# Head norm of the prompt moved from the last stage into the sample mLSTM; decode with two score banks and one pair of key banks

## The chip, the core and the metric

The kernel runs on one core of one Trainium2 chip. The metric is the device time of one execution in microseconds; the median of three runs stands for the kernel. A profile of one execution goes with it: every instruction with its engine, its start and its duration. PE is TensorE, DVE VectorE, ACT ScalarE, POOL GpSimd, SP SyncE, whose queue starts the DMAs.

## What is computed

One step of a hybrid decoder layer. A prompt of 512 tokens (16 learned meta tokens before it) and 8 decode sequences of 4 tokens pass one input projection. Half of the width goes to 8 heads of differential attention (the decode sequences read 32 pages of 128 old keys and values each), half to 4 heads of an mLSTM with a matrix memory. Each head's output is normed, the mLSTM heads are gated, then come the output projection with a residual and an MLP:

```python
def mlstm_output(h, og, g):
    B, T = h.shape[:2]
    hn = rms_norm(h, g)
    o = jax.nn.sigmoid(og.astype(jnp.float32)).reshape(B, T, N_HEADS_M, HEAD_DIM_M)
    return (hn * o).reshape(B, T, MLSTM_WIDTH).astype(og.dtype)

def finish_layer(x, a_heads, m_out, lam_init, attn_out_norm, w_out, norm_ffn, w_up, w_down):
    B, T, _ = x.shape
    a = (rms_norm(a_heads, attn_out_norm) * (1.0 - lam_init)).reshape(B, T, ATT_WIDTH)
    x = x + jnp.concatenate([a.astype(x.dtype), m_out.astype(x.dtype)], axis=-1) @ w_out
    hf = rms_norm(x, norm_ffn) @ w_up
    return x + jnp.square(jax.nn.relu(hf)) @ w_down
```

Here `m_out` is the normed head times the sigmoid of its gate `og`, and `rms_norm` divides by the root of the mean square over a head's 128 (attention) or 256 (mLSTM) values and multiplies by a gain.

## The kernel before

The kernel is a row of stages with a barrier between them: setup, input projection, prompt attention, mLSTM features, prompt mLSTM, `sample_mlstm`, `decode_attention`, `finish_and_project`, `mlp`, `emit`. Each engine has its own list of instructions in a fixed order; semaphores (`wait_ge`, `then_inc`) tie them together. All activations lie transposed, features on partitions and tokens in columns; `mix` holds the 16 chunks of 128 features of all heads (8 attention chunks, then two for each mLSTM head). A matmul with full precision is three passes, low part times high, high times low, high times high (`exact_passes`), so every operand is split into a leading and a trailing part, by ScalarE and VectorE.

`sample_mlstm` runs over the four mLSTM heads for the decode sequences. SP loads four heads' inputs and states (lines 1293 to 1297), then writes the new states as they come (line 1301). For each head TensorE makes the numerators with 16 matmuls of two passes each (`sums`, L1426), then updates the states with 16 more (L1458), which VectorE adds (L1379). ScalarE takes the absolute value of the denominator (L1402), VectorE divides (`divide`, L1348 to L1354), TensorE turns the result back.

`decode_attention` goes through 128 slots of two pages (the loop variable `s`) and some more to drain. In a slot TensorE transposes the keys of page 2s in two halves of four heads each (`turn(s, 0, 0)`, `turn(s, 0, 1)`, L1627), multiplies values of nine slots before (`values`, L1677 to L1688), sometimes transposes probabilities (L1703) and makes the factors (L1713, L1720), transposes page 2s+1 (`turn(s, 1, ...)`) and makes the scores of slot s-1 (`scores`, L1645 to L1650). ScalarE copies the transposed keys out as leading part (`k_high`, L1928), VectorE subtracts for the trailing part (`k_low`, L1770). VectorE also reads the upper half of the scores with their bias (`take`, L1780), ScalarE the lower half (`slower`), GpSimd adds both (`take_slow`, L1608) and makes the trailing part of the values (`v_low`, L1599). The keys' transposes go to four PSUM banks, a pair for each page of a slot; the scores have one. The order on VectorE in a slot:

```python
                if s < PAIRS:
                    k_low(s, 0, 0)
                if 2 <= s < PAIRS + 2:
                    take(s - 2)
                if s < PAIRS:
                    k_low(s, 0, 1)
                ...
                if s < PAIRS:
                    k_low(s, 1, 0)
                    k_low(s, 1, 1)
                if done:
                    cut(v // PPU)
```

Between the second and the third come the trailing part of the probabilities (L1805) and, once a sample, the mixers (L1859); behind the last, in one slot of four, `cut` and `keep` (L1818, L1825), and at times a copy of the queries (L1759, L1764).

`finish_and_project` squares all 16 chunks on VectorE (L2167), sums them over partitions on TensorE (L2231), takes the root on ScalarE and the reciprocal on VectorE (L2183), spreads the inverse over the partitions on TensorE (L2241), multiplies (L2194) and splits (L2127, L2187) chunk by chunk; the gates are loaded and their sigmoid taken meanwhile (L2119, L2173). Only then does the output projection begin (L69 to L71, from `pe_tile`), tile by tile of 128 output features. After the split SP loads the residual over `mix` (L2067); the first tile's sum is added to it.

## Time and profile before

| | us |
|---|---|
| median of 3 runs | 3865.28 |
| lowest and highest | 3864.36, 3869.47 |
| the profiled execution | 3864.66 |
| its span in the trace | 3862.6 |
| mean granted clock of TensorE | 0.959 |

Busy over the span: PE 3595.9 us (93%), DVE 1808.7 (47%), ACT 1280.9 (33%), POOL 713.8 (18%). Times in the rows below are counted from the span's start. A busy PE is not a PE at its peak, as matmuls overlap; a granted clock of 1.00 is 2.4 GHz, 0.50 is 1.2 GHz.

### The profile page before, as it was taken

To read this page: it belongs to the slowest core of one execution; us is meant where nothing else is said; L and a number is where in the kernel's file an instruction comes from. 1 tells how busy PE (TensorE), PEld (TensorE's weight loads), DVE (VectorE), ACT (ScalarE), POOL (GpSimd) and SP (SyncE) were. 2 spreads that over 40 slices of the span, in tenths; PEclk is the share of its full clock that TensorE was granted. 3 is DMA by queue.
4 is the path that set the end of the run, shared out by engine and by line. 5 is a ranking of instruction groups with operands and counts; after the bars stand their busy time and mean duration, and the time that the engine had idled before them with its cause. 6 is when DMAs were issued, how large, how long until landed. Compare 5 with 4: busy or idle time off the path is not lost. (4 is left out here: it accounts for less than half of the span.)

```text
span 3862.6 us, 65521 instructions
## 1 busy us (share of the span) xinstructions
PE 3595.9 (93%) x26234; PEld 3328.7 (86%) x26234; DVE 1808.7 (47%) x2749; ACT 1280.9 (33%) x1879; POOL 713.8 (18%) x436
## 2 busy tenths in 40 slices
PE   7999998866789999999977999999999999999998
PEld 7999996545658888888846999999999999999998
DVE  4222223764447777777765343333333333333333
ACT  3111111432107777777752232222222222222221
POOL 0000000000005888888870000000000000000000
PEclk9999999768869999999988999999999999999999
DMA  7443332115548899999964322222222222222221
GB/s 206 111 111 106 105 107 87 51 53 170 115 152 315 319 327 328 331 326 329 327 210 124 87 75 88 88 88 88 88 88 88 88 88 88 88 88 88 88 88 58
DMA packets 454169, 564.77 MB, mean 146 GB/s; under 512 B 39462, under 2 KB 330196, under 8 KB 453388
## 3 DMA queue, kind: packets, MB, share of 16 engines
q1 hardware_dynamic: 453932, 561.47, 45.3%
q8 instruction: 166, 2.72, 0.3%
q14 instruction: 71, 0.58, 0.0%
HBM read 514.93 MB, written 46.47 MB: 145 GB/s over the span
## 5 line engine op out<-in xcount | busy, mean ns | idle before, releaser
L1599 POOL TENSOR_TENSOR dc_vl<-dc_vpages,dc_vh 128x1024 fp32r<-128x1024 f32 x256 | 609.0, 2395 | 19.0 <-ACT dc_vh L1928 18.6
L69 PE MATMUL f_acc<-hidden_hi,ffn_lo 128*128 128x272 f32 x2048 | 591.7, 289 | 2.8 <-DVE mix_t L2353 2.8
L71 PE MATMUL f_acc<-xf_hi,ffn_hi 128*128 128x272 f32 x2048 | 594.1, 290 | 0.0
L71 PE MATMUL f_acc<-hidden_hi,ffn_hi 128*128 128x272 f32 x2048 | 592.9, 290 | 0.0
L69 PE MATMUL f_acc<-xf_hi,ffn_lo 128*128 128x272 f32 x2048 | 591.0, 289 | 1.0 <-DVE xf_lo L2375 0.4
L70 PE MATMUL f_acc<-hidden_lo,ffn_hi 128*128 128x272 f32 x2048 | 590.7, 288 | 0.0
L70 PE MATMUL f_acc<-xf_lo,ffn_hi 128*128 128x272 f32 x2048 | 588.5, 287 | 0.0
L69 PE MATMUL z_acc<-xn_hi,win_lo 128*128 128x280 f32 x1536 | 447.6, 291 | 1.1 <-DVE win_lo L302 1.1
L71 PE MATMUL z_acc<-xn_hi,win_hi 128*128 128x280 f32 x1536 | 448.5, 292 | 0.0
L2304 ACT ACTIVATE ffn_hi<-ffn_raw 128x2048 fp32r<-128x2048 f32 x127 | 242.3, 1908 | 619.4 <-PE f_acc L71 619.4
L70 PE MATMUL z_acc<-xn_lo,win_hi 128*128 128x280 f32 x1536 | 447.3, 291 | 0.0
L1770 DVE TENSOR_TENSOR dc_kl<-dc_pk,dc_kh 128x512 fp32r<-128x512 f32 x512 | 337.7, 681 | 151.9 <-ACT dc_kh L1928 151.4
L69 PEld LDWEIGHTS f_acc<-hidden_hi,ffn_lo 128*128 128x128 f32 x2048 | 384.5, 188 | 6.4 <-DVE mix_t L2353 6.4
L69 PEld LDWEIGHTS f_acc<-xf_hi,ffn_lo 128*128 128x128 f32 x2048 | 385.7, 188 | 4.3 <-DVE xf_lo L2375 3.6
L70 PEld LDWEIGHTS f_acc<-xf_lo,ffn_hi 128*128 128x128 f32 x2048 | 386.6, 189 | 0.0
L70 PEld LDWEIGHTS f_acc<-hidden_lo,ffn_hi 128*128 128x128 f32 x2048 | 386.0, 188 | 0.0
L71 PEld LDWEIGHTS f_acc<-xf_hi,ffn_hi 128*128 128x128 f32 x2048 | 385.4, 188 | 0.0
L71 PEld LDWEIGHTS f_acc<-hidden_hi,ffn_hi 128*128 128x128 f32 x2048 | 384.9, 188 | 0.0
L2358 DVE TENSOR_TENSOR ffn_lo<-ffn_raw,ffn_hi 128x2048 fp32r<-128x2048 f32 x127 | 291.2, 2293 | 150.8 <-ACT ffn_hi L2304 150.8
L2353 DVE TENSOR_TENSOR mix_t<-mix_t,f_acc 128x544 f32<-128x544 f32 x256 | 182.9, 720 | 362.1 <-PE f_acc L71 362.1
L1928 ACT ACTIVATE dc_kh<-dc_pk 128x512 fp32r<-128x512 f32 x512 | 278.4, 596 | 127.3 <-PE dc_pk L1627 126.3
L69 PEld LDWEIGHTS z_acc<-xn_hi,win_lo 128*128 128x128 f32 x1536 | 289.4, 188 | 1.3 <-DVE win_lo L302 1.3
(359 smaller groups left out, 6248.8 us busy)
## 6 DMA issues: line engine op xcount, KB each, us to landing
dc_kpages<-in_cache_k SPq DMA_DIRECT2D x256, 512.0 KB, 5.4
dc_vpages<-in_cache_v SPq DMA_DIRECT2D x256, 512.0 KB, 5.2
ffn_raw<-in_w_up SPq DMA_DIRECT2D x64, 1024.0 KB, 6.4
ffn_raw<-in_w_down SPq DMA_DIRECT2D x64, 1024.0 KB, 5.0
win_raw<-in_w_in SPq DMA_DIRECT2D x48, 1024.0 KB, 6.1
ffn_raw<-in_w_out SPq DMA_DIRECT2D x16, 1024.0 KB, 6.3
z_scratch<-z_out SPq DMA_DIRECT2D x48, 280.0 KB, 2.4
sm_c<-in_state_C SPq DMA_DIRECT2D x32, 256.0 KB, 4.5
```

The lines of the kernel that those rows point to most:

```text
L69: nc.tensor.matmul(out, wlo, xhi, start=first, stop=False)
L70: nc.tensor.matmul(out, whi, xlo, start=False, stop=False)
L71: return nc.tensor.matmul(out, whi, xhi, start=False, stop=last)
L1599: G.tensor_tensor(vl[:, m % VBUF, :], vring[:, m % RING, :], vh[:, m % VBUF, :].bitcast(F32), ALU.subtract).then_inc(vlo, 1)
L1770: V.tensor_tensor(kl[:, k, hs, i * P:(i + 1) * P], pk[i][half][:, :].rearrange("p (h t) -> p h t", h=HH), kh[:, k, hs, i * P:(i + 1) * P]. ...
L1928: A = lambda out, x, **more: nc.scalar.activation(out, x, ACT.Copy, **more)
L2304: nc.scalar.activation(flow.hi[:, i % 2, :], flow.raw[:, i % G, :], ACT.Copy).then_inc(flow.hi_made, 1)
L2353: nc.vector.tensor_tensor(halves(xt[:, oc, :]), halves(xt[:, oc, :]), acc[2 + i % 2][:, :, 0:d.ohalf], ALU.add).then_inc(added, 1)
L2358: nc.vector.tensor_tensor(flow.lo[:, i % 2, :], flow.raw[:, i % G, :], flow.hi[:, i % 2, :].bitcast(F32), ALU.subtract).then_inc(flow.lo_m ...
```

## The change

In the sample stage the squares, the sums over partitions, the inverse root, the gates and the multiplication by gain and inverse are now done for the 512 columns of the prompt. The inverse goes to DRAM and comes back spread over the partitions by 12 broadcast DMAs. `num` has one bank instead of two, to make room for the sums. In the last stage only the 32 columns of the decode sequences are normed; the split goes over the first half of the columns and then the second; the first weight tile is loaded first; the residual comes in four pieces. In the decode the scores go to two banks in turn, and a slot's two pages share one pair of key banks.

```diff
@@ sample_mlstm
+                if h == 1:
+                    for i in range(d.hm):
+                        sp.dma_start(og[i][:, :, :], ogv[cog // E + i][:, :, N_META:TP]).then_inc(og_in[i], 16)
...
             for h in range(d.hm):
+                if h == d.hm - 1:
+                    sp.wait_ge(inv_made, 1)
+                    sp.dma_start(inv_dram, inv[:, :]).then_inc(inv_out, 16)
+                    sp.wait_ge(inv_out, 16)
+                    for i in range(NH):
+                        sp.dma_start(spread[:, i, :], inv_dram[i:i + 1, :].to_broadcast([P, S])).then_inc(spread_in, 16)
...
+            def gate(h):
+                dve.wait_ge(sigmoid_made, h + 1)
+                dve.wait_ge(squared, d.ha + (h + 1) * E)
+                x = prompt[:, d.ha + h * E:d.ha + (h + 1) * E, :]
+                V.tensor_tensor(x, x, og[h][:, :, :], ALU.mult).then_inc(gated, 1)
+
+            def invert():
+                dve.wait_ge(gathered, d.kc)
+                V.tensor_scalar(root[:, :], mean[0:NH, 0:S], EPS, None, ALU.add).then_inc(rooting, 1)
+                dve.wait_ge(rooted, 1)
+                V.reciprocal(inv[:, :], root[:, :]).then_inc(inv_made, 1)
...
+                V.scalar_tensor_tensor(prompt[:, n, :], prompt[:, n, :], gain, spread[:, head(n), :],
+                                       ALU.mult, ALU.mult).then_inc(normed, 1)
...
+                if h == d.hm - 2:
+                    invert()
+                    for i in range(d.hm):
+                        gate(i)
                 dve.wait_ge(state_new, E * NB * (h + 1))
                 V.tensor_copy(nbh(ncols[:, :, :])[:, :, :, h], c0[h][:, :, :, MD]).then_inc(new_put, 1)
+            for n in range(d.kc):
+                norm(n)
...
+                for n in part(h):
+                    if n >= 6:
+                        act.wait_ge(gathered, n - 5)
+                    nc.scalar.activation(sq[n % 6][:, :], prompt[:, n, :], ACT.Square).then_inc(squared, 1)
...
-                if h >= 2:
-                    pe.wait_ge(divided, h - 1)
+                if h:
+                    pe.wait_ge(divided, h)
...
+                for n in part(h):
+                    pe.wait_ge(squared, n + 1)
+                    pe.wait_ge(gather_made, 3)
+                    x = head(n)
+                    nc.tensor.matmul(mean[0:NH, 0:S], gather[:, int(n >= d.ha), NH - 1 - x:2 * NH - 1 - x], sq[n % 6][:, :],
+                                     start=(n == 0), stop=(n == d.kc - 1)).then_inc(gathered, 1)
@@ decode_attention
-        pk = [[ps(f"dc_pk{i}{half}", [P, 512]) for half in range(2)] for i in range(2)]
+        pk = [ps(f"dc_pk{half}", [P, 512]) for half in range(2)]
-        pscore = ps("dc_pscore", [P, 512])
+        pscores = [ps(f"dc_pscore{i}", [P, 512]) for i in range(2)]
...
-                if n >= 2:
-                    pe.wait_ge(klo, 2 * n - 3 + half)
+                if n >= 1:
+                    pe.wait_ge(klo, 2 * n - 1 + half)
...
-                if s >= 1:
-                    pe.wait_ge(half_biased, s + s // (PG // 2))
-                    pe.wait_ge(slow_out, s)
+                pscore = pscores[s % 2]
+                if s >= 2:
+                    pe.wait_ge(half_biased, s - 1 + (s - 1) // (PG // 2))
+                    pe.wait_ge(slow_out, s - 1)
@@ finish_and_project
+            sp.dma_start(tile(flow.raw, 0), w[:, :, 0:P]).then_inc(flow.landed[0], 16)
+            sp.dma_start(og[:, :, :], ogv[:, :, d.tp:d.t]).then_inc(og_in, 16)
...
+            for i in range(4):
+                rows = slice(i * QUAD, (i + 1) * QUAD)
+                sp.wait_ge(lo_made, N + (i + 1) * QUAD)
+                sp.dma_start(xt[:, rows, :], x[:, rows, :]).then_inc(residual_in, 16)
...
+            for n in range(N // 2):
+                split(0, n)
+            act.wait_ge(og_in, 16)
+            nc.scalar.activation(og[:, :, :], og[:, :, :], ACT.Sigmoid).then_inc(sigmoid_made, 1)
             act.wait_ge(rooting, 1)
             nc.scalar.activation(root[:, :], root[:, :], ACT.Sqrt).then_inc(rooted, 1)
+            act.wait_ge(flow.landed[0], 16)
+            leading(0)
+            for n in range(N // 2, N):
+                split(0, n)
+            act.wait_ge(scaled, 3)
+            for n in range(N):
+                split(1, n)
+                if n == N // 2:
+                    act.wait_ge(flow.landed[1], 16)
+                    leading(1)
...
                     if first and j == 0 and h == 0:
                         pe.wait_ge(lo_made, k + 1)
+                    elif first and j == 0:
+                        pe.wait_ge(lo_made, N + k + 1)
```

The other users of the score bank (`double`, `combine`, `mixers`, `place`) take the bank of slot s-1. `trail` on VectorE follows `split`, and a weight's `trailing` stands before the samples' norm (tile 0) and amid the second half (tile 1).

## Rows read from the trace of the kernel before

**Rows 1.** Busy time by stretch: us, each engine, PE clock, DMA share, GB/s.
```profile
core 0: us, PE busy (x) PEld busy (x) DVE busy (x) ACT busy (x) POOL busy (x), PEclk, DMA share, GB/s
1042.00:1150.00 108.00, 85.70 (x292) 49.49 (x292) 45.28 (x149) 1.55 (x8) 0.77 (x5) 0.67 0.51 162
1200.00:1950.00 750.00, 716.35 (x5145) 612.23 (x5144) 580.13 (x1029) 584.16 (x974) 638.32 (x353) 1.00 0.92 330
```
**Rows 2.** Timeline, last stage: start, duration, engine, line, operation, [idle before <- releaser].
```profile
2014.80 0.34 SPq L2055 DMA_DIRECT2D fh_gains<-in_attn_out_norm  x1
...
2080.80 0.81 PE L69 MATMUL o_acc<-mix_hi,ffn_lo 128*128 128x272 f32 x1
...
2093.92 1.92 ACT L2094 ACTIVATE ffn_hi<-ffn_raw 128x2048 fp32r<-128x2048 f32 x1 [8.76 <-PE o_acc L71]
...
2099.51 0.72 DVE L2145 TENSOR_TENSOR mix_t<-mix_t,o_acc 128x544 f32<-128x544 f32 x1 [13.59 <-DMA mix_t<-xt_scratch]
```
**Rows 3.** Timeline of PE, sample stage: the numerators of heads 2 and 3.
```profile
1100.08 9.97 PE L1426 MATMUL sm_num<-sm_c,sm_qpad 128*32 128x257 f32 x32
...
1124.53 9.70 PE L1426 MATMUL sm_num<-sm_c,sm_qpad 128*32 128x257 f32 x32
```
**Rows 4.** Waits of PE, 1180 to 1950: us in total, times, longest.
```profile
PE dc_pscore L1647 <- DVE dc_scores L1780: 24.7, 38, 1.2
PE dc_pk L1627 <- DVE dc_kl L1770: 8.1, 7, 1.2
```
**Rows 5.** Timeline of PE and DVE in a slot with a late `take`.
```profile
1537.47 1.09 PE L1627 MATMUL dc_pk<-ident,dc_kpages 128*128 128x128 f32 x8
1539.02 0.36 PE L1647 MATMUL dc_pscore<-dc_kh,dc_qhl 128*128 128x256 f32 x1 [0.46 <-DVE dc_scores L1780]
...
1537.75 0.68 DVE L1770 TENSOR_TENSOR dc_kl<-dc_pk,dc_kh 128x512 fp32r<-128x512 f32 x1
1538.35 0.41 DVE L1780 SCALAR_TENSOR_TENSOR dc_scores<-dc_pscore,dc_bias 64x256 f32<-64x256 f32 x1
1538.68 0.68 DVE L1770 TENSOR_TENSOR dc_kl<-dc_pk,dc_kh 128x512 fp32r<-128x512 f32 x1
```
**Rows 6.** Timeline of DVE and PE around the mixers.
```profile
1593.93 5.76 DVE L1859 TENSOR_SCALAR dc_mixer<-dc_comb,dc_factor 128x32 f32<-128x32 f32 x4
1599.61 1.28 DVE L1770 TENSOR_TENSOR dc_kl<-dc_pk,dc_kh 128x512 fp32r<-128x512 f32 x2
...
1600.43 1.16 PE L1627 MATMUL dc_pk<-ident,dc_kpages 128*128 128x128 f32 x8 [1.14 <-DVE dc_kl L1770]
```
**Rows 7.** Timeline of DVE and PE behind an exponential of ACT.
```profile
1551.31 1.29 DVE L1770 TENSOR_TENSOR dc_kl<-dc_pk,dc_kh 128x512 fp32r<-128x512 f32 x2 [1.99 <-ACT dc_kh L1928]
...
1551.91 1.03 PE L1627 MATMUL dc_pk<-ident,dc_kpages 128*128 128x128 f32 x8
```
**Rows 8.** Timeline of PE in a slot at the start of the decode.
```profile
1169.35 1.91 PE L1627 MATMUL dc_pk<-ident,dc_kpages 128*128 128x128 f32 x16
1171.88 0.36 PE L1647 MATMUL dc_pscore<-dc_kh,dc_qhl 128*128 128x256 f32 x1 [0.63 <-DVE dc_scores L1780]
```
**Rows 9.** Timeline of PE, last stage: sums of two rows of squares over partitions.
```profile
2048.55 2.01 PE L2231 MATMUL fh_spread<-fh_sq,fh_gather 128*12 128x272 f32 x8 [1.75 <-DVE fh_sq L2167]
```
**Rows 10.** Groups by line, 2014 to 2081: busy us, mean ns of one, idle before.
```profile
L2194 DVE SCALAR_TENSOR_TENSOR mix_t<-mix_t,fh_gains,fh_spread 128x544 f32<-128x544 f32 x13 | 10.1, 775 | 3.3 <-PE fh_spread L2241 3.3
...
L2173 DVE TENSOR_TENSOR mix_t<-mix_t,fh_og 128x1088 f32<-128x1088 f32 x4 | 5.2, 1292 | 17.6 <-ACT fh_og L2119 17.5
L2139 DVE TENSOR_TENSOR ffn_lo<-ffn_raw,ffn_hi 128x2048 fp32r<-128x2048 f32 x2 | 4.6, 2285 | 0.0
...
L2183 DVE RECIPROCAL fh_inv<-fh_root 12x544 f32<-12x544 f32 x1 | 3.5, 3541 | 0.7 <-ACT fh_root L2124 0.7
```
**Rows 11.** DMA issues: times, KB each, median us from issue to landing.
```profile
ffn_raw<-in_w_out SPq DMA_DIRECT2D x16, 1024.0 KB, 6.3
sm_c<-in_state_C SPq DMA_DIRECT2D x32, 256.0 KB, 4.5
```
**Rows 12.** Timeline: the sample stage's last work on DVE, the next stage's first.
```profile
1145.20 0.49 DVE L1389 COPY sm_nrows<-sm_acc 32x128 f32<-32x128 f32 x2 [0.49 <-PE sm_acc L1466]
...
1149.72 1.16 POOL L1577 MEMSET dc_line<- 1x8 f32 x8 [106.42 <-POOLq L87]
```

More of the change, by code:

```diff
@@ L1252, in sample_mlstm @@
         out = sb("sm_out", [TS, MD])
+        NH, S = d.ha + d.hm, d.seq
+        prompt = mix[:, :, N_META:TP]
+        sq = [sb(f"ph_sq{i}", [P, S]) for i in range(6)]
+        og = [sb(f"ph_og{h}", [P, E, S]) for h in range(d.hm)]
+        gather = sb("ph_gather", [P, 2, 2 * NH - 1])
+        root, inv = sb("ph_root", [NH, S]), sb("ph_inv", [NH, S])
+        spread = sb("ph_spread", [P, NH, S])
+        gains = sb("ph_gains", [P, 1 + E])
+        gather_made, gains_in, inv_out, spread_in = (sems(f"ph_{x}") for x in (
+            "gather_made", "gains_in", "inv_out", "spread_in"))
+        og_in = [sems(f"ph_og_in{h}") for h in range(d.hm)]
+        squared, gathered, sigmoid_made, gated, rooting, rooted, inv_made, normed = (sems(f"ph_{x}") for x in (
+            "squared", "gathered", "sigmoid_made", "gated", "rooting", "rooted", "inv_made", "normed"))
+        cog = (3 * d.aw + 2 * d.mw) // P
+        ogv = z_dram[0:(cog + d.hm * E) * P, :].rearrange("(c e p) t -> c p e t", e=E, p=P)
+        part = lambda h: range(min(6 * h, d.kc), min(6 * h + 6, d.kc))
+        head = lambda n: n if n < d.ha else d.ha + (n - d.ha) // E
         nrows = sb("sm_nrows", [NB * d.hm, MD])
@@ L1257, in sample_mlstm @@
         score = ps("sm_score", [P, 512])
-        num = [ps(f"sm_num{i}", [P, 512]) for i in range(2)]
+        num = ps("sm_num", [P, 512])
+        mean = ps("ph_mean", [P, 512])
         turned = ps("sm_turned", [P, 512])
@@ L1712, in double @@
                 scores_taken(s)
-                nc.tensor.matmul(pscore[:, 0:CHUNKS], twice[:, :], fac[:, :], start=True, stop=True).then_inc(doubled, 1)
+                nc.tensor.matmul(pscores[(s - 1) % 2][:, 0:CHUNKS], twice[:, :], fac[:, :], start=True, stop=True).then_inc(doubled, 1)
             def combine(b, s):
@@ L2162, in _ @@
             V.memset(sumsq[:, :], 0.0).then_inc(sumsq_zeroed, 1)
-            order = list(range(d.ha, d.kc)) + list(range(d.ha))
-            for i, n in enumerate(order):
-                if i >= 2:
-                    dve.wait_ge(summed, i - 1)
-                V.tensor_tensor(sq[i % 2][:, :], mix[:, n, :], mix[:, n, :], ALU.mult).then_inc(squared, 1)
-                if i % 2 and i // 2 < d.hm:
-                    h = i // 2
-                    dve.wait_ge(sigmoid_made, h + 1)
-                    dve.wait_ge(squared, i + 1)
-                    x = mix[:, d.ha + h * E:d.ha + (h + 1) * E, :]
-                    V.tensor_tensor(x, x, og[:, h % 2, :, :], ALU.mult).then_inc(gated, E)
-                if i in (9, 11):
-                    trailing(dve, (i - 9) // 2, (i - 9) // 2)
+            V.tensor_tensor(ssq[:, :, :], smp, smp, ALU.mult).then_inc(squared, 1)
@@ L2176, in _, with trail @@
+            def trail(x, n):
+                dve.wait_ge(hi_made, x * N + n + 1)
+                V.tensor_tensor(mlo[:, n, columns[x]], mix[:, n, columns[x]], mhi[:, n, columns[x]].bitcast(F32),
+                                ALU.subtract).then_inc(lo_made, 1)
+            for n in range(N // 2):
+                trail(0, n)
             dve.wait_ge(gains_in, 32)
             V.tensor_scalar(gains[:, 0:1], gains[:, 0:1], 1.0 - LAM_INIT, None, ALU.mult).then_inc(gated, 1)
-            dve.wait_ge(gated, d.hm * E + 1)
@@ L2179, in _ @@
-            dve.wait_ge(summed, d.kc)
-            V.tensor_scalar(two(root[:, :]), mean[0:NH, :, 0:d.ohalf], EPS, None, ALU.add).then_inc(rooting, 1)
+            dve.wait_ge(summed, 1)
+            V.tensor_scalar(root[:, :], means[0:NH, 0:TS], EPS, None, ALU.add).then_inc(rooting, 1)
+            dve.wait_ge(sigmoid_made, 1)
+            V.tensor_tensor(smp[:, d.ha:N, :], smp[:, d.ha:N, :], og[:, :, :], ALU.mult).then_inc(gated, 1)
             dve.wait_ge(rooted, 1)
-            dve.wait_ge(consts, 6)
@@ L2183, in _ @@
-            V.reciprocal(inv[0:NH, :], root[:, :]).then_inc(inverted, 1)
-            def trail(n):
-                dve.wait_ge(hi_made, n + 1)
-                V.tensor_tensor(mlo[:, n, :], mix[:, n, :], mhi[:, n, :].bitcast(F32), ALU.subtract)\
-                    .then_inc(lo_made, 1)
-            for n in range(d.kc):
-                h = head(n)
-                gain = gains[:, 0:1] if n < d.ha else gains[:, 1 + (n - d.ha) % E:2 + (n - d.ha) % E]
-                dve.wait_ge(spread_ready, h + 1)
-                V.scalar_tensor_tensor(two(mix[:, n, :]), two(mix[:, n, :]), gain, spread[h % 2][:, :, 0:d.ohalf],
-                                       ALU.mult, ALU.mult).then_inc(scaled, 1)
-                if n >= 1:
-                    trail(n - 1)
@@ L2198, in _ @@
-            trail(d.kc - 1)
+            V.reciprocal(inv[:, :], root[:, :]).then_inc(inverted, 1)
+            trailing(dve, 0, 0)
+            dve.wait_ge(gated, 2)
+            dve.wait_ge(spread_ready, 1)
+            rows = lambda lo, hi: spread[:, lo * TS:hi * TS].rearrange("p (h t) -> p h t", t=TS)
+            V.scalar_tensor_tensor(smp[:, 0:d.ha, :], smp[:, 0:d.ha, :], gains[:, 0:1], rows(0, d.ha),
+                                   ALU.mult, ALU.mult).then_inc(scaled, 1)
+            heads_m = smp[:, d.ha:N, :].rearrange("p (h e) t -> p e h t", e=E)
@@ L2199, in _ @@
+            for e in range(E):
+                V.scalar_tensor_tensor(heads_m[:, e], heads_m[:, e], gains[:, 1 + e:2 + e], rows(d.ha, NH),
+                                       ALU.mult, ALU.mult).then_inc(scaled, 1)
+            for n in range(N // 2, N):
+                trail(0, n)
+            for n in range(N):
+                trail(1, n)
+                if n == N // 2:
+                    trailing(dve, 1, 1)
             dve_group(dve, 0, True)
```

139 lines of the change are left out of this document (72 added, 67 removed).

## The prediction

> **What bounds the kernel now.** I read the busy times by stretch first, because the change touches three stages and leaves all before and behind them as it is. In [rows 1] the reader sees that in the decode TensorE is busy in 716 of 750 us at the full clock, with GpSimd at 638, VectorE at 580 and the DMA engines at 0.92: TensorE sets the pace there, and whatever stops it for a moment is paid. The stage of the sample mLSTM holds TensorE for 86 of 108 us at a mean clock of 0.67. Next the timeline where the last stage of the three begins [rows 2]: it starts at 2014.80, its first output matmul at 2080.80, so 66.0 us go to the head norm and the split before the output projection runs; ScalarE is freed by the end of the first output tile at 2093.92, and the residual has landed at 2099.51, some 6 us before the second tile ends. In the sample stage each head begins with 32 matmuls of some 10 us [rows 3] in which the other engines wait. Last the waits of TensorE in the decode [rows 4]: 24.7 us in 38 waits for `take` (the read of the scores), 8.1 us in 7 for `k_low`. The first is what the second score bank removes, the second what the lost pair of key banks touches.
>
> **Decode, the part with two signs.** I call a slot one pass of the loop (two pages), 128 in all; 16 are one sample, and from the second sample on the timeline repeats itself sample by sample. Now the scores of a slot need `take` of the slot before; after the change they need the one before that, which is long done, so this wait of 24.7 us goes. But a page's transposes now wait for `k_low` of the page just before, same half, and not of two pages before. On VectorE `take` stands between the two `k_low` of a slot's first page. So where `take` is late, the second `k_low` is later still, and the transposes of the second page now wait for it, with scores, values and the next slot queued behind them on TensorE. Slot at 1533.95 [rows 5]: `take` ends at 1538.76 and the scores start 0.26 later, at 1539.02. The second `k_low` ends at 1539.36. A transpose starts 0.14 after the `k_low` it waits for (1600.29 to 1600.43 in [rows 6]), the scores 0.36 after the last four transposes begin. After: 1539.36 + 0.14 + 0.36 = 1539.86, which is +0.84 us where 0.70 were to be won (without any wait the scores would start at 1538.32).
>
> There are six such slots in a sample (38 waits over some 7.3 samples are 5 to 6). Walked through one sample, slot by slot, by the ends of `k_low` in the timeline: two that stand alone give +0.85 each. Two neighbours give +1.3 together, as VectorE's own chain there is only 0.4 later. The one behind the mixers: VectorE sits 5.76 us in four tiny multiplies there, and TensorE waits 1.14 for `k_low` [rows 6], but only after it has done the next slot's first transposes and values. After the change it waits before these 2.3 us of work; the score wait of that slot goes, and GpSimd, one slot behind, has had 0.75 more time by then: +0.9 with the slot after. The one behind a blocked copy of the queries gets nearly all back in the same way: +0.05. And where ScalarE's exponential holds back the last two `k_low` of a slot [rows 7], the next slot's transposes, which now need them (they end near 1552.0 and at 1552.6, while the transposes begin at 1551.91 now), slip: +0.4. Sum 0.85 + 0.85 + 1.3 + 0.9 + 0.05 + 0.4 = 4.35 us a sample, times 7.3 = 32 us.
>
> The eight slots before the values begin are bare chains of transposes, `k_high`, `k_low` and scores, and the scores, 2.53 us behind the slot's start, are held 0.63 by `take` [rows 8]. By the same step each grows 0.85; the very first, whose second page now waits for the first page's late `k_low`, by 2.4: 8 x 0.85 + 2.4 = 9 us. Decode: +32 + 9 = **+41 us**. Bounds: if nothing comes back through GpSimd, 6.0 a sample and 53 in all; if half of the late slots are covered by work that I count as serial, 25; if the key waits were all hidden, the whole 24.7 would be a gain.
>
> **Sample stage, where the prompt's norm goes.** ScalarE's 16 squares (0.6 us each) fall into its waits for TensorE. The 16 sums over partitions are two matmul passes of 512 columns each: by [rows 9], 8 passes of 272 columns take 2.01 us at full clock with the run-out of the last, 0.23 apart, hence 0.43 for 512 columns and 32 x 0.43 = 14 us, twice that at half. They stand on TensorE between one head's updates and the next head's 32 matmuls, with nothing beside them. Those 32 begin slowly now (9.97 us where 32 passes of 257 columns make 7 at the rate of [rows 9]): the clock is low after the updates. The sums will take over that slow stretch and the 32 run fast behind them, so I take +14 us, with 27 as the upper end. In the third head VectorE then has the root's input (0.7), the wait for ScalarE's root (0.8), the reciprocal of 12x512 (3.5 x 512/544 = 3.3) and four gates (1.2 each by the 1.29 of 1088 columns) [rows 10]: 9.7 us, against 7 of matmuls and the absolute value that cover them: +2.7. The gates wait on VectorE ahead of the last head's division, which lets the updates go; hence it counts. At the end of the stage come 16 multiplications of 512 columns on VectorE with nothing left to hide them: 0.775 each of 544 with overlap, 0.65 apart, +10.4. They need the inverse through DRAM and back: a write, then 12 broadcasts of 256 KB on SP's queue ahead of the last head's 8 stores; a 256 KB load lands in 4.5 us [rows 11], the 12 at the rate of the states in some 12 to 14, from 1145 + 2 on in the new order, about when VectorE is free at 1160: +1. The stage's end hangs on the last copy of VectorE plus 4.0 us, from 1145.69 to 1149.72 [rows 12], as before. The other new loads (4 x 512 KB of the gate and the gains) pass the states of heads 2 and 3 on SP's queue by some 8 us; these are needed 30 us later. If that slack were gone it would cost 8. Stage: 14 + 2.7 + 10.4 + 1 = **+28 us**, from 23 to 42.
>
> **Finish stage.** SP issues the first weight tile first. It lands about 6.3 us after the issue [rows 11]; behind it come the 128 KB gate of the samples and the gains, I take it by 9 (a 256 KB load that lands in 4.5 is the nearest row; the first tile and these share the engines). VectorE and ScalarE split the first 8 rows meanwhile. Then a root and a reciprocal of 32 columns (1 us), the leading part of the weights (1.92 [rows 2]) and the trailing part (2.29 [rows 10]): first output matmul 14.2 us after the start against 66.0, -51.8. It starts on a cold clock and meets one `trailing` amid the second half: +2.5. The residual now goes in four pieces from 19 us on, 13.6 us as now, so until 35; the add that needs it must come by 38. If it were 5 us late, 2 would be lost. Finish: **-49 us**, from -52 to -44.
>
> **The sum.** +41 + 28 - 49 = +20. The profiled execution took 3864.66 us (span 3862.6), 0.6 under the median of 3865.28: 3864.7 + 20 = **3885 us**.
>
> **Rivals.** (1) *The two score banks win*: the wait of 24.7 us goes and the new waits for keys lie under values and scores, as they do in the ten slots where `take` is early. For it: 24.7 us measured, TensorE the bound. Against: the order on VectorE in [rows 5], in which the second `k_low` ends 0.6 after `take`. It decides as soon as that `k_low` is done before the transposes are due; then decode gives -25, all -46: 3819. The Trainium skill's page PSUM — Partial Sum Buffer, in its summary of rules for kernel authors, speaks for this rival: to read a bank while matmuls run, send them to a different bank. By that rule alone the time would be this rival's; it does not speak of the banks that are taken away for it. Chance 0.06. (2) *The key waits cancel the score waits*, decode +-5: 3864.7 + 28 - 49 = 3844. Chance 0.07. (3) *A colder clock in the decode*: the wait behind the mixers becomes one of 3.3 us before any work, and the low clock of the sample stage (0.67 with gaps, against 1.00 in the decode, [rows 1]) shows what gaps do. If each sample then runs 4 us of work at half rate, 7 x 2 = 14, and as much in the chain at the front: 3885 + 14 to 28 = 3899 to 3913. The page TensorE: Matmul & The Clock Gate, section on HAM oscillation, of the Trainium skill has waits inside a loop put the clock back to half in every pass; whether these are long enough no row here shows. Chance 0.17. (4) *The norm is moved, not hidden*: sums at half clock, spread late, residual late: sample +40, finish -44, 3902; chance 0.10, and a part of it is in (3) too. Forecast as summed: 0.60.
>
> A measurement of this kernel tells 0.2% (8 us) from no change. Faster than 3857: (1), (2): 0.13. Within: the low end of the forecast, decode near +25: 0.09. Slower: 0.78. The range goes from 3860 to 3914.
>
> **What would show it.** Right: no wait of the score matmuls for `take`, and instead waits of the transposes for `k_low`, some 6 a sample, each sample 4 to 6 us longer; the first scores 3.4 us behind their slot's start; the sample stage at 133 to 138 us instead of the 108 of [rows 1]; the first output matmul 14 us into the last stage. Wrong: a decode sample no longer than now, or transposes that never wait; a sample stage whose last matmul comes less than 10 us later, with the sums hidden; a second output tile that waits for the residual.

## The result, and the profile after

| kernel | median, us | ratio to the kernel before, 95% interval |
|---|---|---|
| before (19 runs beside the changed kernel's) | 3865.8 | |
| changed (19 runs) | 3872.9 | 1.0019 [1.0012, 1.0026] |
| forecast | 3885 (3860 to 3914) | |

The change costs 7.1 us by the medians, where 20 were forecast; the two profiled executions are 10.4 apart (span 3873.0 against 3862.6). The sign and the stages came as forecast, the size did not, and most of the thirteen us that are missing come from what GpSimd does in the decode. First the stages. Windows of the changed kernel, the sample stage and the stretch of the decode that answers to [rows 1] (columns as there):

```profile
core 0: us, PE busy (x) PEld busy (x) DVE busy (x) ACT busy (x) POOL busy (x), PEclk, DMA share, GB/s
1042.00:1176.00 134.00, 100.87 (x324) 52.72 (x324) 64.36 (x171) 18.05 (x31) 0.68 (x5) 0.69 0.53 170
1200.00:1950.00 750.00, 700.68 (x4977) 593.88 (x4976) 541.07 (x989) 569.16 (x940) 598.67 (x334) 0.99 0.89 316
```

The sample stage lasts 134.2 us (1041.86 to 1176.04) instead of 107.3. In the decode every engine has less to do in the same 750 us, TensorE 701 instead of 716: the decode runs slower, and no engine took the time by working. Not all of these 15 us are waits, as the decode also begins 26 us later in this stretch; e1 below, with the old decode behind the same sample stage, has 711. The timeline of the last stage answers to [rows 2] (start, duration, engine, line, operation, what ended the idle time before):

```profile
2077.16 0.39 SPq L2139 DMA_DIRECT2D ffn_raw<-in_w_out  x1
...
2080.92 1.88 PE L2319 MATMUL fh_means<-fh_sample_sq,fh_gather 128*12 128x32 f32 x32 [7.36 <-POOL fh_scatter L2173]
...
2091.52 0.59 PE L69 MATMUL o_acc<-mix_hi,ffn_lo 128*128 128x272 f32 x1
...
2096.97 6.79 SPq L2151 DMA_DIRECT2D mix_t<-xt_scratch  x4
...
2112.17 0.72 DVE L2236 TENSOR_TENSOR mix_t<-mix_t,o_acc 128x544 f32<-128x544 f32 x1 [8.81 <-DMA mix_t<-xt_scratch]
```

The first output matmul comes 14.36 us into the stage (2091.52 less 2077.16), where it took 66.0. VectorE waits 8.8 us for the residual, until 35 us into the stage; the second output tile does not wait for it.

The waits of TensorE in the decode, 1200 to 1950 (us in total, times, longest), answer to [rows 4]; the kernel before has 22.2 us for `take` and 8.1 for `k_low` in the same stretch. This is the whole answer:

```profile
PE dc_pk L1707 <- DVE dc_kl L1851: 46.9, 87, 1.2
```

The score matmuls wait for `take` no more, and the transposes wait for `k_low`, which is what was forecast. Slot 13 of a sample shows how, as [rows 5] did before (timeline of DVE and PE):

```profile
1795.77 0.67 DVE L1851 TENSOR_TENSOR dc_kl<-dc_pk,dc_kh 128x512 fp32r<-128x512 f32 x1
1796.37 0.40 DVE L1862 SCALAR_TENSOR_TENSOR dc_scores<-dc_pscore,dc_bias 64x256 f32<-64x256 f32 x1
1796.70 0.67 DVE L1851 TENSOR_TENSOR dc_kl<-dc_pk,dc_kh 128x512 fp32r<-128x512 f32 x1
...
1796.58 0.63 PE L1707 MATMUL dc_pk<-ident,dc_kpages 128*128 128x128 f32 x4 [1.03 <-DVE dc_kl L1851]
1797.42 0.66 PE L1707 MATMUL dc_pk<-ident,dc_kpages 128*128 128x128 f32 x4 [0.21 <-DVE dc_kl L1851]
1797.83 0.36 PE L1728 MATMUL dc_pscore<-dc_kh,dc_qhl 128*128 128x256 f32 x1
```

`take` stands between the two `k_low`, the second four transposes start 0.05 after the second `k_low` ends (1797.37 to 1797.42), the scores 0.41 behind them: they start 1.06 after `take` has ended, where before they started 0.26 after it.

Now the slots one by one. This table is worked out from the starts of each slot's first transposes in the timeline of TensorE: the time from one slot to the next, us, the median over six samples (the second to the seventh), for the slots in which these kernels differ. "Sample" is the sum of all 16. The kernels of the experiments stand in it too.

| slot of the sample | 0 | 3 | 4 | 5 | 6 | 7 | 8 | 9 | 10 | 11 | 13 | 15 | sample |
|---|---|---|---|---|---|---|---|---|---|---|---|---|---|
| before | 7.27 | 5.47 | 6.89 | 7.40 | 5.91 | 8.31 | 7.07 | 6.40 | 6.31 | 5.91 | 7.02 | 5.47 | 102.4 |
| changed | 7.42 | 5.73 | 7.45 | 7.81* | 6.77 | 5.78 | 7.20 | 7.22 | 6.31 | 6.70 | 7.83 | 5.70 | 104.9* |
| e3, take last | 7.42 | 5.73 | 7.11 | 7.76 | 9.99 | 7.91 | 7.07 | 6.90 | 6.80 | 6.37 | 7.50 | 5.70 | 109.3 |
| e4, three key banks | 7.27 | 5.48 | 6.76 | 7.40 | 5.91 | 11.14 | 7.07 | 6.31 | 6.31 | 5.88 | 6.90 | 5.47 | 105.3 |
| e6, norm, new mixers | 7.27 | 5.47 | 6.88 | 7.41 | 5.91 | 5.48 | 7.06 | 6.41 | 6.31 | 5.91 | 7.01 | 5.48 | 99.6 |
| e9, GpSimd gives way | 7.27 | 5.47 | 6.89 | 7.40 | 5.92 | 5.95 | 7.07 | 6.40 | 6.31 | 5.92 | 7.02 | 5.47 | 100.1 |
| e8, take first | 7.27 | 5.47 | 6.29 | 7.38 | 5.91 | 5.48 | 7.07 | 6.32 | 6.30 | 5.47 | 6.47 | 5.68 | 98.0 |

(* Where TensorE keeps its full clock. In four of these six samples it fell in slot 5, which then lasts 9.05 to 9.38 and the sample 106.4; more on this below.)

Slots 3, 4, 5, 9, 13, 15 and 0 grew as forecast. Slot 7 did not: it became 2.5 us *shorter*, and slot 11 grew by 0.8, where 0.05 was forecast. Both have to do with GpSimd. The timeline of POOL, ACT and DVE at the mixers, in the changed kernel:

```profile
1748.44 0.74 POOL L1688 TENSOR_TENSOR dc_scores<-dc_scores,dc_slow 64x256 f32<-64x256 f32 x1
1749.14 2.39 POOL L1679 TENSOR_TENSOR dc_vl<-dc_vpages,dc_vh 128x1024 fp32r<-128x1024 f32 x1
1751.90 2.37 POOL L1679 TENSOR_TENSOR dc_vl<-dc_vpages,dc_vh 128x1024 fp32r<-128x1024 f32 x1 [0.37 <-ACT dc_vh L2010]
...
1750.76 1.06 ACT L2010 ACTIVATE dc_vh<-dc_vpages 128x1024 fp32r<-128x1024 f32 x1
...
1749.40 2.60 DVE L1941 TENSOR_SCALAR dc_mixer<-dc_comb,dc_factor 128x32 f32<-128x32 f32 x4
1751.92 1.28 DVE L1851 TENSOR_TENSOR dc_kl<-dc_pk,dc_kh 128x512 fp32r<-128x512 f32 x2
```

and of POOL and ACT in the kernel before, at the mixers of [rows 6]:

```profile
1593.78 0.72 POOL L1608 TENSOR_TENSOR dc_scores<-dc_scores,dc_slow 64x256 f32<-64x256 f32 x1
1594.46 4.75 POOL L1599 TENSOR_TENSOR dc_vl<-dc_vpages,dc_vh 128x1024 fp32r<-128x1024 f32 x2
...
1595.29 1.06 ACT L1928 ACTIVATE dc_vh<-dc_vpages 128x1024 fp32r<-128x1024 f32 x1
```

Before, GpSimd runs two `v_low` back to back to 1599.21, and the four mixers end at 1599.69. In the changed kernel GpSimd is 0.8 us sooner by its slot's start (the slots start at 1590.51 and 1745.98, the first `v_low` 3.95 and 3.16 behind them). So it is through with the first `v_low` at 1751.53, before ScalarE's next `v_high` ends at 1751.82. It stands still for 0.37 us, and in this gap the mixers get through: 2.60 us instead of 5.76.

### The profile page after: what moved, and what is told of

Its sections match the earlier page's. It is cut to its first block and busy times, and to the rows that moved or that the text cites. A ratio compares the mean times of both kernels' runs of the same rounds, so it can differ in the third digit from the quotient of the medians.

```text
span 3873.0 us, 65571 instructions
## 1 busy us (share of the span) xinstructions
PE 3599.4 (93%) x26210; PEld 3329.6 (86%) x26210; DVE 1785.6 (46%) x2757; ACT 1302.6 (34%) x1916; POOL 714.8 (18%) x438
## 5 line engine op out<-in xcount | busy, mean ns | idle before, releaser
L1707 PE MATMUL dc_pk<-ident,dc_kpages 128*128 128x128 f32 x2048 | 286.6, 279 | 59.7 <-DVE dc_kl L1851 57.4
```

The lines of the kernel that those rows point to most:

```text
L1707: mm = nc.tensor.transpose(pk[half][:, j * P:(j + 1) * P], kring[:, n % RING, h * P:(h + 1) * P], c.ident[:, :])
```

## The experiments

Every time is the median; the ratio is to the kernel before on the same chip. "Norm alone" means the changed kernel with the decode of the kernel before.

| run | us | ratio [95% interval] |
|---|---|---|
| e1, norm alone | 3842.8 | 0.9942 [0.9928, 0.9956] |
| e2, decode alone | 3894.2 | 1.0073 [1.0059, 1.0087] |
| e5, changed, new mixers | 3864.8 | 0.9998 [0.9989, 1.0007] |
| e6, norm alone, new mixers | 3820.0 | 0.9883 [0.9868, 0.9898] |
| e3, changed, take last | 3896.2 | 1.0079 [1.0065, 1.0092] |
| e4, changed, three key banks | 3860.7 | 0.9989 [0.9980, 0.9998] |
| e7, e4 with the new mixers | 3820.3 | 0.9881 [0.9866, 0.9896] |
| e8, e6 with take first | 3807.6 | 0.9851 [0.9836, 0.9866] |
| e9, norm alone, GpSimd gives way | 3826.0 | 0.9900 [0.9885, 0.9915] |
| e10, changed, GpSimd gives way to the queries | 3862.5 | 0.9994 [0.9985, 1.0003] |
| e11, e8 with keep later | 3807.1 | 0.9850 [0.9837, 0.9864] |
| e12, changed, short sums | 3855.9 | 0.9975 [0.9965, 0.9985] |

**The two halves of the change.** e1 takes `decode_attention` from the kernel before, all else from the changed one; e2 the other way round.

> The moved norm with the decode as it was: two pairs of key banks, one score bank. Traces of both kernels put 26.1 us more before the decode's first slot and 51.9 us less behind the decode in the changed kernel. Theory G (the decode change costs about as forecast, less what GpSimd's catching up gives back): -25.9, so 3840 us, from 3837 to 3845, and the decode's slots as long as in the kernel before. Rival S (the sizes of the moved norm were right as forecast, and the decode alone was too dear in the forecast): 28 - 49 = -21, so 3845. Rival K (what the two parts give depends on each other, by the clock the decode is entered with): the decode's slots differ from the kernel before by more than 3 us in all.

> The decode with two score banks and one pair of key banks, the norm left where it was. Theory G: the decode and its tail grow by 36 us in the one profile of the changed kernel, of which some 6 are a clock that fell in one slot of four samples; so +30 to +36, 3896 to 3902 us, with mixers of some 2.6 us on VectorE in place of 5.8 in each sample. The forecast as it stood: +41, 3907, with mixers of 5 us. Rival K: with the decode entered in another way the growth differs from that of the changed kernel by more than 4 us.

Measured: -22.9 and +28.5 us. The forecast had -21 and +41, so the moved norm was sized well and the whole miss lies in the decode. The parts add up: -22.9 + 28.5 = +5.6, against 7.1 for both, so they do not depend on each other by more than the measurement can tell. In e1's trace the slots of a sample are those of the kernel before (102.5 us), in e2's those of the changed one (104.9 at the full clock), and e2's mixers are as short as there (712 ns each on average, 1506 before). e2 came out 1.5 below the least that theory G gave it. One small part does depend on the moved norm: the first nine slots of the decode take 47.1 us in e1, with the old decode, and 44.2 in the kernel before.

**Do the mixers decide?** In e5 and e6 one instruction makes all mixers, with the factors read from PSUM:

```diff
-                V.tensor_copy(factor[:, :], pscores[(s - 1) % 2][:, 0:CHUNKS]).then_inc(mixed, 1)
-                dve.wait_ge(mixed, 2 * b + 1)
-                for i in range(CHUNKS):
-                    ins = V.tensor_scalar(mixer[:, i, :], comb[:, :], factor[:, i:i + 1], None, ALU.mult)
-                ins.then_inc(mixed, 1)
+                V.tensor_tensor(mixer[:, :, :], <factors in PSUM, spread over t>, <comb, spread over i>,
+                                ALU.mult).then_inc(mixed, 2)
```

> The changed kernel, with the mixers made by one VectorE instruction that reads the doubled factors from PSUM, in place of a copy and four multiplications with both operands in SBUF. VectorE instructions with a PSUM operand show no block by GpSimd in either trace. Theory G: the mixers take 0.3 us instead of 2.6; the keys of that slot come up to 2 us sooner, of which the slot gives back 0.9: 7 x 0.9 = 6, so 3866 us. Rival C (the mixers' length doesn't matter for what the change costs): 3866 as well, or 3873; the pair with the next run decides.

> The moved norm with the decode as it was, and with the mixers in one VectorE instruction from PSUM, as in the run before. Theory G: the 5.8 us that VectorE sits in the mixers go; the slot behind them falls from 8.3 to some 5.6 us: 7 x 2.7 = 19, so 19 below the run with the norm alone, near 3821. The change of the banks then costs more than it did: the run before minus this one is 45 us, where changed kernel minus norm alone is 30 to 33. Rival C (the mixers were not what the slot behind them waited for): within 5 us of the norm alone, and the difference between the two runs is the same 30 to 33.

Measured: 3864.8 and 3820.0. The groups of DVE between 1200 and 1950 in e6 (count, then busy us and mean ns of one):

```profile
L1936 DVE TENSOR_TENSOR dc_mixer<-dc_pscore,dc_comb 128x128 f32<-128x128 f32 x7 | 2.0, 292 | 2.8 <-issue 2.4 <-PE dc_pscore L1793 0.4
```

The mixers take 0.29 us, slot 7 falls from 8.3 to 5.48, and the difference between the two decodes grows from 30 (3872.9 - 3842.8) to 44.8 us. With nothing to give back, the change of the banks costs 104.0 - 99.6 = 4.4 us a sample, of which the waits that the forecast named in slots 3 to 5, 9, 13, 15 and 0 make 3.2, slot 11 makes 0.8 and slots 7 and 8 make 0.4. So GpSimd paid back some 15 us of the change's price.

**Push GpSimd back again.** e3 moves `take` behind both `k_low`, possible as the second score bank leaves it the time:

```diff
-                if 2 <= s < PAIRS + 2:
-                    take(s - 2)
                 if s < PAIRS:
                     k_low(s, 0, 1)
+                if 2 <= s < PAIRS + 2:
+                    take(s - 2)
```

> The changed kernel, with VectorE's read of the scores (take) behind both k_low of the first page instead of between them; the second score bank leaves it the time. Theory T (the transposes wait because take stands ahead of the second k_low): in the five late slots of a sample (4, 5, 9, 11, 13) the transposes of the last half start 0.33 us sooner, the length of a take: 5 x 0.33 x 7.3 = 12, and 8 x 0.33 = 3 in the slots before the values; 3873 - 15 = 3858 us. Rival G: take 0.6 us later holds GpSimd back by as much, its v_low reach into the mixers again, and the block of 5.8 us comes back: 3858 + 7 x 3 = 3879, with mixers over 5 us.

Measured: 3896.2, rival G and more. The table shows both halves: slots 4, 9, 11 and 13 lose the 0.33 that theory T gives them, slots 6 and 7 grow by 5.4. The timeline of POOL, DVE and PE at the mixers of e3:

```profile
1759.79 0.72 POOL L1688 TENSOR_TENSOR dc_scores<-dc_scores,dc_slow 64x256 f32<-64x256 f32 x1
1760.48 4.68 POOL L1679 TENSOR_TENSOR dc_vl<-dc_vpages,dc_vh 128x1024 fp32r<-128x1024 f32 x2
...
1759.96 5.67 DVE L1941 TENSOR_SCALAR dc_mixer<-dc_comb,dc_factor 128x32 f32<-128x32 f32 x4
...
1766.38 1.94 PE L1707 MATMUL dc_pk<-ident,dc_kpages 128*128 128x128 f32 x8 [3.76 <-DVE dc_kl L1851]
```

With `take` 0.6 us later GpSimd is late again, its two `v_low` close up, the mixers take 5.67, and TensorE waits 3.76 us before the next slot's first transposes: it is the wait "of 3.3 us before any work" of the forecast's third rival. The clock falls there as that rival said: the windows of e3's slots 6 and 7, PEclk the third figure from the end, show 0.92 and 0.67.

```profile
1756.40:1766.38 9.98, 6.11 (x44) 5.11 (x43) 8.22 (x11) 4.45 (x7) 8.76 (x5) 0.92 0.87 311
1766.38:1774.28 7.90, 7.90 (x40) 6.70 (x41) 4.25 (x10) 5.69 (x9) 3.06 (x2) 0.67 0.58 206
```

**Take away the lost bank.** e4 gives the halves a ring of three banks:

```diff
-        pk = [ps(f"dc_pk{half}", [P, 512]) for half in range(2)]
+        pk = [ps(f"dc_pk{i}", [P, 512]) for i in range(3)]
...
-                if n >= 1:
-                    pe.wait_ge(klo, 2 * n - 1 + half)
+                m = 2 * n + half
+                if m >= 3:
+                    pe.wait_ge(klo, m - 2)
```

with `pk[m % 3]` in the transposes, `k_high` and `k_low`; e7 is e4 with the new mixers.

> The changed kernel, with the turned halves in a ring of three banks instead of two (two score banks and three key banks fill all eight with the rest): a half waits for the k_low three halves before, not two. Theory T (all of the decode's cost is this wait of the transposes): the last half of a page pair needs the first k_low of its slot, which ends 0.9 us sooner, and starts without delay; the late slots are as long as in the kernel before or 0.1 shorter. But with the late slots gone GpSimd is as late as before, the mixers block VectorE 5.8 us again, and the slot behind them grows by some 0.7, as its second transposes need the previous slot's third k_low. Sum: within 5 of the norm alone, 3838 to 3848 us. Rival B (something else than the bank makes the slots longer, the pages' loads or the second score bank): 3855 or more.

> The run with three key banks, and the mixers in one VectorE instruction from PSUM. Theory T: the late mixers gone, neither the scores nor the transposes wait any more: 0.1 to 0.7 us shorter in each of six late slots than with the norm, the old decode and the new mixers (3820): 7.3 x (0.6 to 3) = 4 to 22, so 3798 to 3816. Rival B: 3820 or more.

Measured: 3860.7 and 3820.3. By the time alone e4 falls to rival B, but its trace shows the late slots back at the times of before or 0.1 below, and one slot that takes the rest: slot 7, at 11.1 instead of 8.3. I had priced the blocked mixers at +0.7 there, as in a ring of three the second transposes of the slot wait for the third `k_low` of the slot before, ahead of the values (3.4 us in each sample). Windows of slot 7 in the second and the fourth sample:

```profile
1315.11:1324.17 9.06, 5.66 (x42) 4.88 (x41) 7.32 (x14) 4.92 (x9) 5.70 (x4) 1.00 0.95 347
1523.14:1534.77 11.63, 8.23 (x42) 6.82 (x41) 8.27 (x15) 5.73 (x9) 6.02 (x5) 0.71 0.82 299
```

In the second sample, the only one in which TensorE kept its full clock, the slot takes 9.07, 0.8 more than before, which is the price. In the six that follow the clock fell to 0.84 or 0.71 in this slot, and it takes 10.4 to 11.9; that is 12.6 us in all, without which e4 would be at 3848, the upper end of theory T. With the mixers out of GpSimd's way this is gone, and e7 is as fast as e6, no faster: 3820.3 against 3820.0, so theory T failed there. Two score banks and three key banks stand against one and four, and nothing is won. TensorE's longest waits in total between 1200 and 1950, in e6 and then in e7:

```profile
PE dc_pscore L1727 <- DVE dc_scores L1860: 18.3, 34, 1.2
PE dc_pk L1708 <- DVE dc_kl L1852: 16.1, 35, 1.1
```

The wait changed its name.

**The order instead of the bank.** e8 keeps the old banks and puts `take` first:

```diff
+                if 2 <= s < PAIRS + 2:
+                    take(s - 2)
                 if s < PAIRS:
                     k_low(s, 0, 0)
-                if 2 <= s < PAIRS + 2:
-                    take(s - 2)
-                if s < PAIRS:
                     k_low(s, 0, 1)
```

> The moved norm, the decode's banks as they were (two pairs of key banks, one score bank), the mixers in one instruction from PSUM, and take ahead of the first k_low of the slot instead of between the two. Theory T: the wait of the scores for take, 18.3 us in 34 waits between 1200 and 1950 us in the run with these mixers and take in its old place, and some 5 us in the slots before the values, goes without a second score bank, as take ends 0.6 us sooner: 3820 - 23 = 3797 us. Rival V (VectorE's later k_low then holds the transposes or ScalarE): 3810 or more.

> The run with take first (3807.6 us), with the reduction `keep` (2.0 us on VectorE, once in four slots) moved from the end of its slot to the middle of the next one, behind both k_low of the first page. Theory L (the late slots are late since keep stands ahead of take and k_low): the scores of slots 4, 9 and 13 of a sample no longer wait, some 0.3 to 0.4 us each, 7.3 x 1 = 7, so 3800 us. Rival P (take is early enough since it is first, and TensorE sets the pace of these slots): 3805 or more, or slower, where the second page's k_low come late instead.

Measured: 3807.6, between the two theories. TensorE's waits between 1200 and 1950 in e8:

```profile
PE dc_pout L1758 <- issue: 6.2, 7, 0.9
PE dc_pscore L1727 <- ACT dc_slow L2006: 2.7, 6, 0.9
PE dc_pk L1707 <- DMA dc_kpages<-in_cache_k: 0.7, 2, 0.4
PE dc_pk L1707 <- DVE dc_kl L1850: 0.5, 1, 0.5
```

The 18.3 us for `take` are gone, and 12.4 of the time. Slots 4, 11 and 13 give 0.4 to 0.6 each; slot 5 gives nothing, as its values now start late (6.2 us before `dc_pout`, where e6 has 2.1). e11 moves `keep` behind both `k_low` of the next slot (one call moved); it came out at 3807.1, so rival P: with `take` first these slots are TensorE's own. (Its trace has 0.4 us less a sample, but in slots 5 and 15, not in 4, 9 and 13.)

**GpSimd gives way.** Two runs leave all work as it is and add one wait a sample to GpSimd, before its second `v_low` of the slot: in e9 (norm alone) for the mixers, in e10 (changed kernel) for the copy of the queries.

```diff
+                    u, at = s // PPU - 2, s % PPU
+                    if i == 1 and at == 2 and 0 <= u < UNITS and last_of_sample(u):
+                        pool.wait_ge(mixed, 2 * (u // CHUNKS) + 2)
```

(e10: at the slot of `lay`, `pool.wait_ge(q_laid, 2 * b + 2)`.)

> The moved norm with the decode as it was and the mixers as they were; GpSimd alone is told to wait, once a sample, for the end of the mixers before the second v_low of that slot. Theory Q (VectorE's mixers are blocked for as long as GpSimd has v_low ready back to back, so by whole v_low of 2.4 us, and a gap between two of them lets the mixers through): the mixers fall from 5.8 to some 2.7 us, the slot behind them from 8.3 to 5.5, 7 x 2.8 = 20, so 3843 - 20 = 3823 us, as near to 3820 as with the mixers from PSUM, though no work was taken away. Rival D (GpSimd's delay costs as much in the values behind it as it gives): 3838 or more.

> The changed kernel; GpSimd waits once a sample for the copy of the next sample's queries (two VectorE copies in SBUF, 2.2 us in the trace, of which v_low blocks some 1.9) before the second v_low of that slot. Theory Q: the copy takes some 0.3 us, the first k_low of the next slot (11 of a sample) is no longer late, and that slot falls from 6.7 to 5.5 us: 7 x 1.2 = 8, so 3873 - 8 = 3865 us. Rival D: 3870 or more.

Measured: 3826.0 and 3862.5. The group of the mixers in e9 (28 instructions are seven samples, 3.4 us each, from 5.8):

```profile
L1942 DVE TENSOR_SCALAR dc_mixer<-dc_comb,dc_factor 128x32 f32<-128x32 f32 x28 | 24.0, 920 | 0.2
```

and of the copies of the queries in e10 (two a sample; mean 171 ns, from 1096 in the changed kernel):

```profile
L1843 DVE COPY dc_q<-dc_qs 64x32 f32<-64x32 f32 x14 | 2.4, 171 | 0.2
```

To make GpSimd wait made the kernel 17 us faster in e9 and 10 in e10. Theory Q holds here: what VectorE paid was the queue of `v_low`, by whole instructions. Of the 10 us of e10 the slots explain 7.3 x 0.83 = 6; its profile also has none of the falls of the clock in slot 5, which cost the changed kernel's profile some 6 us.

**The sums of the sample stage.** e12 leaves 15 of the 16 sums at one column:

```diff
+                    wide = 1 if n else S
-                    nc.tensor.matmul(mean[0:NH, 0:S], ..., sq[n % 6][:, :],
+                    nc.tensor.matmul(mean[0:NH, 0:wide], ..., sq[n % 6][:, 0:wide],
```

> The changed kernel, with 15 of the 16 sums over partitions in the sample stage cut to one column of 512 (the prompt's means then hold the first of the 16 squares alone). In the changed kernel the sums take 6.7, 6.3 and 6.0 us, and the numerators behind them 7.7 us each, where they took 9.3, 10.5 and 10.2 before. Theory N (the sums only take over the stretch that runs at the low clock): with the sums down to some 1 us a head the numerators go back to 9.3 to 10.5, so 15 saved and 7 lost: 3865 us. Rival F (the numerators are faster for another reason, as the single bank or their order): they stay at 7.7, 3857 us.

Measured: 3855.9, which by the time alone speaks for rival F; the trace decides otherwise. The timeline of PE, sums and numerators of the second head in the changed kernel:

```profile
1077.89 6.84 PE L1542 MATMUL ph_mean<-ph_sq,ph_gather 128*12 128x512 f32 x12
1084.57 7.12 PE L1500 MATMUL sm_num<-sm_c,sm_qpad 128*32 128x257 f32 x32
```

and of the third head in e12:

```profile
1101.93 0.45 PE L1543 MATMUL ph_mean<-ph_sq,ph_gather 128*12 128x1 f32 x12
1102.24 9.96 PE L1500 MATMUL sm_num<-sm_c,sm_qpad 128*32 128x257 f32 x32
```

Without the long sums the numerators are slow again (9.96, the figure of [rows 3]); the sums of the changed kernel take the slow stretch on themselves, as theory N says. That the whole gained more than 8 us has two reasons in the trace: the wait of the last updates for VectorE (1.2 us) went, and the updates of the second and the last head ran 1.5 and 1.2 us faster, those of the last at a clock of 0.72 instead of 0.62. By the trace the decode begins 13.0 us sooner and takes 2.0 less, with a clock that fell in slot 5 in three samples instead of four; the rest of the 17 is not explained.

## Why the prediction was right or wrong

**The decode's key waits: right.** Of the waits that it foresaw, two lone slots at +0.85 each came out at +0.82 (9) and +0.81 (13), the neighbours with the slot ahead of them (3 to 5) at +1.22 for 1.3, the slot behind ScalarE's exponential (15 and 0) at +0.38 for 0.4. In the slots before the values the first scores start 3.34 us behind their slot's start (3.4 foreseen), and they cost 10.2 us in e2, 11.7 in the changed kernel, for 9 (e1, with the old decode, already has 2.9 there).

**The step that failed** is the pair of terms "the one behind the mixers ... +0.9 with the slot after" and "the one behind a blocked copy of the queries ... +0.05". Both rest on "GpSimd, one slot behind, has had 0.75 more time by then". It did have 0.8. But I took the block as shorter by just that time (mixers of 5 us, as the expectation of e2 has the forecast), and GpSimd is bound on the other side by ScalarE's `v_high`. At the mixers the 0.8 opened a gap of 0.37 between two `v_low`, and the block lost a whole further `v_low`, 3.16 us in all; slots 6 to 8 came out at 0.86 - 2.53 + 0.13 = -1.5 instead of +0.9. At the queries the second `v_low` of the changed kernel waits for `v_high` too, but VectorE comes to the copy only after that wait. The timeline of POOL and DVE there, changed kernel:

```profile
1776.13 2.39 POOL L1679 TENSOR_TENSOR dc_vl<-dc_vpages,dc_vh 128x1024 fp32r<-128x1024 f32 x1
1779.29 2.38 POOL L1679 TENSOR_TENSOR dc_vl<-dc_vpages,dc_vh 128x1024 fp32r<-128x1024 f32 x1 [0.77 <-ACT dc_vh L2010]
...
1779.71 2.21 DVE L1840 COPY dc_q<-dc_qs 64x32 f32<-64x32 f32 x2
```

GpSimd stood still for 0.77 and so could pass nothing on: the copy takes 2.21 us for 2.23 to 2.27 before, and slot 11 grew by 0.79. Together 2.44 less and 0.74 more make 1.7 a sample; over 7.3 samples 12 of the 13 us by which the forecast was too high. A decode of 7.3 x 2.48 + 10.2 = 28.3 is near what e2 measured (+28.5). e3, e5, e6, e9 and e10 each show this cause from another side. That these sums fit to a microsecond is in part luck. They hold no fall of the clock, and e2's profile, 32.6 us above that of the kernel before, has some 6 us of them. In the changed kernel the other misses nearly cancel: the sample stage and the finish came out 4 us below the forecast, the slots before the values 2.7 above, and the falls of the clock, which the sum left out, add some 5 in the profile, net of one fall in the kernel before.

**Sample stage: right.** +26.8 by the trace for +28. The sums take 19.0 us (6.69, 6.35 and 6.00) and give back 7.1 in three stretches of numerators: +12 for +14. VectorE's hold cost 1.2 for 2.7, the 16 multiplications 10.69 for 10.4, the spread nothing for 1. The updates ran 2 to 3 us slower, which the forecast did not have.

**Finish: right, and a little better.** 14.36 us to the first output matmul for 14.2, hence -51.6; the cold clock and the second `trailing`, +2.5 in the forecast, do not show in the sum (from the first output matmul on the kernel is 0.4 us shorter than before). The residual came at 35 us into the stage, as forecast, and held nothing up.

**The rivals.** The second score bank did not win, and e7 shows that it would win nothing even with a third key bank, as long as VectorE keeps its order (with `take` first it was not tried). The key waits did not cancel the score waits: from e6 to e5 the change of the banks costs 44.8 us. The fourth rival's sizes did not come: the sample stage cost 26.8 and not 40, the finish gave 51.6 and not 44. The third rival named a clock that falls behind the mixers: this happens where TensorE waits 3.4 to 3.8 us there, in all seven samples of e3 and in six of seven of e4, but not in the changed kernel, where that wait never came about. Its price of 2 us a sample (4 us of work at half rate) stood on no row; slot 7 takes 2.1 us longer in e3, at a clock of 0.67, than in the changed kernel at 1.00. In the changed kernel the clock fell in slot 5 instead. Windows of that slot in two samples:

```profile
1631.72:1641.10 9.38, 7.98 (x46) 6.69 (x45) 7.31 (x15) 4.95 (x8) 6.87 (x5) 0.82 0.80 276
1738.18:1745.98 7.80, 6.40 (x46) 5.11 (x45) 7.31 (x15) 4.94 (x8) 5.43 (x4) 1.00 0.91 297
```

The waits in slots 4 and 5 are the same in both (0.8 and 1.2 us the longest), and one keeps the clock. It fell in slot 5 in four of seven samples of the profile (some 6 us), in four in e2's, in three in e5's and e12's, in the kernel before once, in a slot 7, and in e10, with the same waits in slots 4 and 5, never. What decides is open. That the two profiles differ by 10.4 and the medians by 7.1 would fit a profiled execution with more such falls than most; this is argued, not shown.

## What to carry to other kernels

Before a wait is moved between buffers, look at what the waiting engines do in their order: here neither bank set the pace but the place of one read in VectorE's sequence, and with that read first the old banks gave 12 us. A delay does not pass through a queue unchanged; ask for every engine that "has more time" what bounds it on the other side, and whether a block comes in whole instructions. e8 and e11, the moved norm with the mixers from PSUM and `take` first, are 1.5% faster than the kernel before, and 1.7% faster than the changed one by the medians.

## What the runs showed of the hardware

VectorE can sit far longer behind GpSimd than one instruction of it. At the end of the decode of the kernel before, a subtraction of 64x4 with both operands in SBUF stands behind seven `v_low` (timeline of POOL and DVE):

```profile
1970.11 16.32 POOL L1599 TENSOR_TENSOR dc_vl<-dc_vpages,dc_vh 128x1024 fp32r<-128x1024 f32 x7
...
1971.10 15.35 DVE L1834 TENSOR_TENSOR dc_eff<-dc_beyond,dc_low 64x4 f32<-64x4 f32 x1
```

It ends at 1986.45, 0.02 after GpSimd has run dry at 1986.43, and no `v_low` boundary on the way let it in. Nor did the boundaries behind the addition and the first `v_low` let the mixers in, in seven samples of the kernel before and seven of e3; the gap of 0.37 us in the changed kernel did, in all seven. But a boundary without a gap is not always closed. The very last mixers of the kernel before stand behind four `v_low` just as close together (1995.12 to 2004.48), and each of the four gets through at the end of one `v_low` (timeline of DVE and POOL, the second and third):

```profile
1997.44 2.42 DVE L1859 TENSOR_SCALAR dc_mixer<-dc_comb,dc_factor 128x32 f32<-128x32 f32 x1
1999.77 2.42 DVE L1859 TENSOR_SCALAR dc_mixer<-dc_comb,dc_factor 128x32 f32<-128x32 f32 x1
...
1997.44 2.38 POOL L1599 TENSOR_TENSOR dc_vl<-dc_vpages,dc_vh 128x1024 fp32r<-128x1024 f32 x1
1999.76 2.39 POOL L1599 TENSOR_TENSOR dc_vl<-dc_vpages,dc_vh 128x1024 fp32r<-128x1024 f32 x1
```

The changed kernel shows the same at its end. What decides between the two is open.

A multiplication of 128x128 with one operand in PSUM took 0.29 us in the place of the mixers (e6). The Trainium skill, page SBUF — State Buffer, section SBUF: two separate sides, has VectorE and GpSimd share one pair of ports under a lock that one instruction holds to its end. By that rule a block comes in whole instructions, and the trace agrees, with mixers of 2.60 us behind one `v_low` and 5.76 behind two and an addition.
